# State-space projection: pairs of channel tiles by seven half products, with sums of weights and of rows

## What is computed

```python
D_INNER, SSD_HEADS, SSD_GROUPS, D_STATE, D_CONV = 2048, 32, 4, 128, 4
XBC_DIM = D_INNER + 2 * SSD_GROUPS * D_STATE      # 3072

def ssd_mixer(h, w_in, conv_w, conv_b, dt_bias, a_log, d_skip, gate_norm, w_out):
    z, xbc, dt = jnp.split(h @ w_in, [D_INNER, D_INNER + XBC_DIM], axis=-1)
    xbc = jax.nn.silu(causal_depthwise_conv(xbc, conv_w, conv_b))
    xs, bm, cm = jnp.split(xbc, [D_INNER, D_INNER + SSD_GROUPS * D_STATE], axis=-1)
    dt = jax.nn.softplus(dt.astype(jnp.float32) + dt_bias.astype(jnp.float32))
    a = -jnp.exp(a_log.astype(jnp.float32))
    y = ssd_chunked_scan(xs, dt, a, bm, cm) + d_skip[:, None] * xs
    y = y.reshape(Bsz, S, D_INNER) * jax.nn.silu(z.astype(jnp.float32))
    ...
```

## Time and profile before

| | |
|---|---|
| three runs | 2775.22 us median (2773.9 to 2781.66) |
| the profiled execution, its own time | 2773.66 us |
| its span, first to last instruction | 2771.9 us |
| mean granted clock of TensorE | 0.978 |
| PE busy over the span | 2646.5 us (95%) |
| DVE / ACT busy over the span | 1865.4 us (67%) / 1610.9 us (58%) |
| projection stage | about 1247 to 1724 us of the span |

### The profile page before, as it was taken

The page is one execution under the profiler, slowest core; times in us unless marked ns, Lnnn a source line. Parts: engine busy times, 40 slices in busy tenths (PEclk is TensorE's granted clock), DMA queues, the critical chain, the costliest instruction groups (busy, mean ns, idle before and its releaser), DMA issues. The chain is left out here.

```text
span 2771.9 us, 40341 instructions
## 1 busy us (share of the span) xinstructions
PE 2646.5 (95%) x13893; PEld 2137.9 (77%) x13893; DVE 1865.4 (67%) x2201; ACT 1610.9 (58%) x2036; POOL 543.3 (20%) x464
## 2 busy tenths in 40 slices
PE   8999999898999999999999999999998999999993
PEld 7886667676888888877788887887885888888882
DVE  6335766537888888876572542786335888888896
ACT  4135555425888888865331222784122888888883
POOL 0000000001334444420000000441000344334440
PEclk9999999998999999999999999999999999999996
DMA  4315110016999999966242323884114999999995
GB/s 167 89 46 183 40 47 24 31 71 247 378 380 379 386 389 383 383 258 208 73 124 69 122 84 133 308 304 144 46 39 157 353 391 383 371 381 379 380 373 233
DMA packets 238390, 619.23 MB, mean 223 GB/s; under 512 B 31976, under 2 KB 76544, under 8 KB 238144
## 3 DMA queue, kind: packets, MB, share of 16 engines
q1 hardware_dynamic: 206992, 558.88, 55.6%
q0 software_dynamic: 19136, 33.61, 3.2%
q10 hardware_dynamic: 12144, 25.17, 2.6%
HBM read 567.08 MB, written 86.13 MB: 236 GB/s over the span
## 5 line engine op out<-in xcount | busy, mean ns | idle before, releaser
L2680 DVE TENSOR_TENSOR moe_w_low<-moes_raw,moe_w_high 128x2048 fp32r<-128x2048 f32 x384 | 865.5, 2288 | 128.9 <-ACT moe_w_high L2609 128.9
L2609 ACT ACTIVATE moe_w_high<-moes_raw 128x2048 fp32r<-128x2048 f32 x384 | 721.8, 1915 | 52.9 <-PEq L155 39.2
L2471 POOL COPY moe_pick<-moes_tokens 128x1 int32 (+1 forms) x64 | 104.1, 1627 | 585.7 <-PE moe_px L2522 580.7
L174 PE MATMUL moe_py<-moe_w_high,moe_h_high 128*128 128x512 f32 x512 | 209.2, 409 | 0.0
L174 PE MATMUL moe_pg<-moe_w_high,moe_x_high 128*128 128x512 f32 x512 | 204.5, 399 | 0.0
L174 PE MATMUL moe_pu<-moe_w_high,moe_x_high 128*128 128x512 f32 x512 | 204.3, 399 | 0.0
L176 PE MATMUL moe_py<-moe_w_high,moe_h_low 128*128 128x512 f32 x512 | 201.1, 393 | 0.0
L176 PE MATMUL moe_pg<-moe_w_high,moe_x_low 128*128 128x512 f32 x512 | 200.9, 392 | 0.0
L176 PE MATMUL moe_pu<-moe_w_high,moe_x_low 128*128 128x512 f32 x512 | 200.8, 392 | 0.0
L175 PE MATMUL moe_py<-moe_w_low,moe_h_high 128*128 128x512 f32 x512 | 199.6, 390 | 0.0
L175 PE MATMUL moe_pu<-moe_w_low,moe_x_high 128*128 128x512 f32 x512 | 199.0, 389 | 0.0
(11 more groups left out here) (444 smaller groups left out, 6119.8 us busy)
## 6 DMA issues: line engine op xcount, KB each, us to landing
moes_raw<-in_w_gate SPq DMA_DIRECT2D x128, 1024.0 KB, 7.6
moes_raw<-in_w_up SPq DMA_DIRECT2D x128, 1024.0 KB, 7.8
moes_raw<-in_w_down SPq DMA_DIRECT2D x128, 1024.0 KB, 8.3
XC<-pre SPq DMA_DIRECT2D x24, 512.0 KB, 5.1
Z<-sproj_z SPq DMA_DIRECT2D x32, 256.0 KB, 2.4
scan_z<-Z SPq DMA_DIRECT2D x32, 256.0 KB, 6.0
YS<-scan_y ACTq DMA_DIRECT2D x32, 256.0 KB, 6.1
y_first<-YS SPq DMA_DIRECT2D x16, 512.0 KB, 3.9
```

What stands on the lines that cost most here:

```text
L174: nc.tensor.matmul(out, lh, rh, start=start, stop=False)
L2471: nc.gpsimd.tensor_copy(pick[a][:, :], M.tokens[:, bass.ds(b, 1)]).then_inc(picked[a], 1)
L2609: nc.scalar.activation(wh[c % SPLIT_SLOTS][:, :], M.raw[j][:, :], ACT.Copy).then_inc(w_high, 1)
L2680: nc.vector.tensor_tensor(wl[j][:, :], M.raw[c % RAW_SLOTS][:, :], bits(wh[j][:, :]), ALU.subtract).then_inc(w_low, 1)
```

## The change

**Seven products instead of eight.** Two tiles of channels (2p and 2p + 1) form a pair. With the contraction cut into two halves of 4 tiles (KH) and the rows into two halves, the pair's result is a 2 x 2 product of half blocks. It took eight half products (each 12 matmuls, four contraction tiles by three passes); now it takes seven, by sums of blocks (the Winograd form of Strassen's scheme). UNITS holds 12 pairs of 7 products (84 units of 12 matmuls) between two gate groups ahead (16 units) and two behind.

**Sums of rows, once.** mix(k), k = 0 to 3, on DVE: four additions that give back whole rows from high and low parts, four subtractions and two low parts, each 128 x 512; ACT makes two high parts. mix_late(j), j = 0 to 3: the high part (ACT) and low part (DVE) of 128 x 1024, into the buffers of the gate weights, free only in the last unit of gate group 1.

**Sums of weights, per pair.** ACT scales both tiles by the gains in 16 instructions of 128 x 128 (gain_tile, in place of DVE's L1472). DVE makes 4 sums (weights_sum). Each of the 7 operands, 128 x 512, gets a high part (ACT, operand_high) and a low part (DVE, operand_low), three products ahead, in a ring of 4.

**Combination, per pair.** The products go to 8 banks in turn. ACT copies the first to e1 (keep_e1), DVE adds the others up in 7 instructions of 128 x 512 (add_u2 to add_c12) into u. The first tap of a convolution is ACT's (tap_first), three stay on DVE. For 8 of the 24 tiles (LATER: the odd tile in two pairs of three) u is stored to XC instead, loaded again during the last two gate groups, and convolved there.

**Room.** acc, c, two of the raw buffers and others now lie in X. So X is stored to a new tensor XS (8 stores of 512 KB, after the additions) and loaded back in the scan (8 loads, at items 20 to 27). sums and step_to_end move from NT + 9 and NT + 12 to NT + 3 and NT + 5. first_operands is issued at NU - 3.

```diff
+    UNITS = [('gate', g, t) for g in range(EARLY) for t in range(NT)]
+    V0 = len(UNITS)
+    UNITS += [('pair', p, q) for p in range(NPAIR) for q in range(PRODUCTS)]
+    V1 = len(UNITS)
+    UNITS += [('gate', g, t) for g in range(EARLY, G) for t in range(NT)]
...
+    WHEN = {NT: range(5, 9), V1 - 4: (9,), V1 - 3: (10,), V1: (11, 12), V1 + NT - 1: range(13, 17)}
...
+    LATER = [2 * p + 1 for p in range(NPAIR) if p % 3 < 2]
...
+    PREPARE = {NT + 2: 0, NT + 4: 1, NT + 5: 2, NT + 6: 3}
...
+            for t in range(NT):
+                sp.wait_ge(added[1], t + 1)
+                sp.dma_start(K.XS[tile(t), :], K.X[:, t, :]).then_inc(x_saved, 16)
...
-                if v == NU - 4:
...
+                if v == NU - 3:
...
+            def product(v):
...
+                if p == 0 and q == 1:
+                    pe.wait_ge(late_low, 2)
+                if p == 0 and q == 3:
+                    pe.wait_ge(late_low, 4)
+                if p == 0 and q >= 4:
+                    pe.wait_ge(mix_low, 2 * KH)
+                pe.wait_ge(op_low, o + 1)
...
+                    last = split_product(nc, out, (h[:, k, :], l[:, k, :]), moving(q, k), k == 0, k == KH - 1)
...
+            def gain_tile(i):
+                act.wait_ge(raw_loaded[buffer_of(('tile', i))], 16 * loads_until(('tile', i)))
+                for k in range(ND):
+                    last = nc.scalar.activation(raw_tile(i)[:, k, :], raw_tile(i)[:, k, :], ACT.Copy, scale=K.vecs[:, V_SSD + k:V_SSD + k + 1])
+                last.then_inc(tile_gained, 1)
+            def operand_high(o):
+                p, n = divmod(o, PRODUCTS)
+                if o >= SLOTS:
+                    act.wait_ge(done, V0 + o - SLOTS + 1)
+                else:
+                    act.wait_ge(x_turned, NT)
+                if n in (0, 2, 5):
+                    act.wait_ge(tile_gained, 2 * p + 2)
+                else:
+                    act.wait_ge(s_ok, 4 * p + {4: 1, 3: 2, 1: 3, 6: 4}[n])
+                high, _ = operand(o)
+                nc.scalar.activation(high, source(o), ACT.Copy).then_inc(op_high, 1)
...
+            def mix(k):
+                for n, (high, x) in enumerate(((T1H, tmp[0]), (T4H, tmp[3]))):
+                    act.wait_ge(mixed, 2 * k + n + 1)
+                    nc.scalar.activation(high[k], x, ACT.Copy).then_inc(mix_high, 1)
...
+            def mix(k):
+                lo, hi = slice(0, HALF), slice(HALF, S)
+                def whole(out, kk, h):
+                    step(V.tensor_tensor(out, bits(K.HH[:, kk, h]), bits(K.HL[:, kk, h]), ALU.add))
+                if k:
+                    dve.wait_ge(mix_low, 2 * k)
+                whole(tmp[0], k, lo)
+                whole(tmp[1], k, hi)
+                whole(tmp[2], KH + k, hi)
+                whole(tmp[3], KH + k, lo)
+                V.tensor_tensor(tmp[0], tmp[1], tmp[0], ALU.subtract).then_inc(mixed, 1)
+                step(V.tensor_tensor(t3f[:, k, :], tmp[2], tmp[1], ALU.subtract))
+                dve.wait_ge(mixed, 2 * k + 1)
+                step(V.tensor_tensor(t2f[:, k, :], tmp[2], tmp[0], ALU.subtract))
+                V.tensor_tensor(tmp[3], tmp[3], t2f[:, k, :], ALU.subtract).then_inc(mixed, 1)
+                dve.wait_ge(mix_high, 2 * k + 1)
+                V.tensor_tensor(T1L[k], tmp[0], bits(T1H[k]), ALU.subtract).then_inc(mix_low, 1)
+                dve.wait_ge(mix_high, 2 * k + 2)
+                V.tensor_tensor(T4L[k], tmp[3], bits(T4H[k]), ALU.subtract).then_inc(mix_low, 1)
...
+            def operand_low(o):
+                dve.wait_ge(op_high, o + 1)
+                high, low = operand(o)
+                V.tensor_tensor(low, source(o), bits(high), ALU.subtract).then_inc(op_low, 1)
+            def weights_sum(p, n):
+                second, first = raw_tile(2 * p), raw_tile(2 * p + 1)
+                lo, hi = slice(0, KH), slice(KH, ND)
+                dve.wait_ge(tile_gained, 2 * p + 1 + (n > 1))
+                if n > 1:
+                    dve.wait_ge(s_ok, 4 * p + n - 1)
+                elif p == 0:
+                    dve.wait_ge(sums_stored, 32)
+                else:
+                    dve.wait_ge(op_low, PRODUCTS * (p - 1) + 5)
...
+                V.tensor_tensor(out, a, b, op).then_inc(s_ok, 1)
...
+                if v in PREPARE:
+                    mix(PREPARE[v])
...
+                if v == V0 - 1:
+                    mix_late(0)
+                    mix_late(1)
+                if v == V0:
+                    mix_late(2)
+                    mix_late(3)
+                p, s = divmod(v - V0, PRODUCTS)
+                here, ahead = 0 <= p < NPAIR, -1 <= p < NPAIR - 1
+                if s == 0 and 0 < p <= NPAIR:
+                    add_c12(p - 1)
+                if here and s == 2:
+                    add_u2(p)
+                if here and s == 4:
+                    add_u3(p)
+                if here and s == 3:
+                    add_c11(p)
+                if here and s == 5:
+                    add_u4(p)
+                    add_c22(p)
+                if here and s == 6:
+                    add_c21(p)
+                if ahead and s == 4:
+                    weights_sum(p + 1, 2)
+                if 0 <= v - V0 + 3 < NPAIR * PRODUCTS:
+                    operand_low(v - V0 + 3)
+                if ahead and s == 3:
+                    weights_sum(p + 1, 1)
+                if ahead and s == 4:
+                    weights_sum(p + 1, 3)
+                if ahead and s == 6:
+                    weights_sum(p + 1, 4)
+                for i, some in convs.get(v, ()):
+                    convolve(i, some)
...
+                if 5 * LOAD <= n < 7 * LOAD:
+                    t = n - 5 * LOAD
+                    sp.dma_start(K.X[:, t, :], K.XS[t * P:(t + 1) * P, :]).then_inc(K.x_back, 16)
```

More of the change, by code:

```diff
@@ L1123, in ssd_project_stage @@
[L1123 to L1134, removed]
@@ new lines, in ssd_project_stage @@
+    SEQ = [i for i in range(NTILES) if i not in LATER] + LATER
+    NOW = NTILES - len(LATER)
+    rank = {i: n for n, i in enumerate(SEQ)}
+    LEADS = 4
+    taps, silus, stores, convs = {}, {}, {}, {}
+    for i in SEQ[:NOW]:
+        v, row = V0 + PRODUCTS * (i // 2 + 1), i % 2
+        taps.setdefault(v, []).append(i)
+        silus.setdefault(v + 2 * (row + 1), []).append(i)
+        stores.setdefault(v + 2 * row + 3, []).append(i)
+        for n, some in enumerate(((1,), (2, 3)) if row else ((1, 2, 3),)):
+            convs.setdefault(v + row + n, []).append((i, some))
@@ new lines, in _ @@
+            load(('piece', 7))
+            load(('piece', 8))
+            sp.wait_ge(x_saved, 16 * NT)
+            sp.wait_ge(scaled, NT)
+            sp.dma_start(tap, A["conv"].rearrange("k p n -> p k n")).then_inc(tap_loaded, 16)
+            for v in range(0, NU + 2):
+                if v == NT + 1:
+                    for i in range(4):
+                        load(('tile', i))
+                if v == V1 + 2:
+                    for n in range(13, 17):
+                        load(('piece', n))
+                p, s = divmod(v - V0, PRODUCTS)
+                if s == 4 and 0 <= p < NPAIR - 2:
+                    load(('tile', 2 * p + 4))
+                    load(('tile', 2 * p + 5))
+                if s == 4 and p in (NPAIR - 2, NPAIR - 1):
+                    for n in range(2):
+                        load(('piece', 9 + n + 2 * (p - NPAIR + 2)))
+                if v == NT + 6:
@@ L1308, in _ @@
                     last.then_inc(dt_done, 1)
-                unit(v)
+                if UNITS[v][0] == 'gate':
+                    gate(v)
+                else:
+                    product(v)
                 if v == NT:
@@ L1422, in _ @@
             for v in range(NU + 2):
-                if v == NT:
-                    act.wait_ge(dt_done, 1)
-                    for h in range(2):
-                        nc.scalar.activation(dts[:, half(h)], pd[h], ACT.Copy).then_inc(dt_kept, 1)
-                if 1 <= v <= NU:
+                if 1 <= v <= NU and UNITS[v - 1][0] == 'gate':
                     evict(v - 1)
@@ new lines, in add_c12, with convolve @@
+            def add_c12(p):
+                ready(p, 6)
+                dve.wait_ge(u4_ok, p + 1)
+                V.tensor_tensor(result(p, 1, 1), bank(p, 6), result(p, 1, 1), ALU.add).then_inc(c12_ok, 1)
+            def convolve(i, taps_now):
+                r, t = rank[i], TILES[i]
+                for n in taps_now:
+                    if n == 1:
+                        dve.wait_ge(first_tap, r + 1)
+                    else:
+                        dve.wait_ge(steps, (CONV - 2) * r + n - 1)
+                    last = V.scalar_tensor_tensor(out=acc[r % 2], in0=u_at_hand(i)[:, n:n + S], scalar=tap[:, t, n:n + 1], in1=acc[r % 2],
```

442 lines of the change are left out of this document (296 added, 146 removed).

## The result

The median went from 2775.22 to 2761.39 us (five runs each side); the ratio is 0.9946, 95% interval 0.9931 to 0.9961. The forecast was 2759, and faster. The profiled execution took 2761.39, its span is 2759.4 against 2771.9, and what differs from the forecast lies at the two ends of the stage, above all at its exit.

The account below looks back on a forecast made before the run. PE (TensorE), busy 30 of 30 us mid-stage, was taken as the bound. Span 2771.9 - 32.6 + 10.2 + 2 + 4 = 2755.5; plus 1.8 (execution) and 1.56 (median) gives 2759 us; range 2744 to 2774.

Parts of the forecast that it names:

- The matmuls removed, -32.6: In the pairs' products: 84 matmuls per pair instead of 96, 144 fewer at 0.2267 us each, saving 32.6 us.
- The pairs at no cost: In the pairs: DVE's mean load of 16.2 us stays under PE's 19.04 and ACT's work is hidden; cost 0.
- Rival (c): In the pairs: DVE becomes the bound and the kernel slower, 2784 us; gain gone from 20.4 us per pair; chance 0.09.
- The handshake on every new instruction: In the pairs on DVE: 0.27 us idle at each of 18 new instructions, 4.9 us more per pair.
- The entry, +10.2 and +2 for the clock: Way into the pairs: DVE's and ACT's queues delay product 1 by 10.2 us; lower clock afterwards costs 2 us.
- rival (a): Entry and exit covered, ACT running ahead and stores sharing the rings; only 3 us lost, 2745.6 us; chance 0.14.
- The exit, +4: Way out to the scan: late first operands and last gate stores queued behind them cost 4 us, bounds 0 and 9.
- The rest at nothing: Saving x, restoring it, third gate group's splits: 0 each, up to 3, 2, 2 us; start's store stalls: 0.5 gain at most.
- The clock within the pairs: In the pairs: the granted clock was expected to hold 1.00 despite a bank change every 12 matmuls instead of 24.
- rival (d): In the pairs: PE falls to the lower clock; a fifth of the matmuls slowed gives 2799 us; chance 0.03.
- The clock behind the idle: Behind PE's idle ahead of product 1: matmuls start 0.43 us apart instead of 0.2267; 2 us, from 0 to 5.

Follow-up runs that it names:

- e8b_dve_more: Changed kernel with each operand's low part subtracted twice on DVE, 84 instructions more; median 2788.29 us, ratio 1.0047 to the kernel before.
- e1: Changed kernel without DVE's wait for the two stores of the sums ahead of pair 0's first sum of weights; median 2758.08 us against 2761.4.
- e9_none_later: Changed kernel with no convolution put behind the pairs, all 24 run in them; median 2753.40 us against 2761.4.
- e2: Changed kernel with all the scan's first operands issued earlier, at gate unit V1+8 of 16; median 2764.43 us against 2761.4.
- e6b: Changed kernel with only the broadcast of the sums issued early, behind gate unit V1+1, three row loads left in place; median 2763.59 us against 2761.4.
- e6: Changed kernel with the broadcast of the sums issued behind gate unit V1+1 and the three row loads at V1+8; median 2762.10 us against 2761.4.
- e11: Changed kernel with the scan's first operands issued behind the last gate store instead of ahead of the last three; median 2766.59 us against 2761.4.
- e4_keep_busy: Changed kernel with 56 useless small transposes on PE while it waits for product 1's operands; median 2761.51 us against 2761.4.
- e3: Changed kernel with mix(0) made ahead of the step sizes in DVE's and ACT's queues; median 2756.61 us against 2761.4.

## Why the prediction was right, and where it was not

**The matmuls removed, -32.6: right.** The page has 144 fewer. With every loss taken away the stretch is 32.9 us shorter.

**The pairs at no cost: right.** DVE's 25.7 of 30 us on the mean over the pairs (1396 to 1606) is 16.3 per pair against 16.2 reckoned, and no product but the first two waits. Rival (c), DVE as the bound, gave a load at which the gain is gone of 20.4; e8b_dve_more at 21.2 is 0.47% slower than before, which fits that point. The handshake on every new instruction, which the rival needed, did not come: it would have shown as idle of DVE between them, and e8b's pace leaves no room for it.

**The entry, +10.2 and +2 for the clock: right, link by link.** Counted from dt, mix(1) ended at 42.7 (43.0 forecast), the wait for the stores at 49.3 (49.4), product 0 started at 58.75 (58.8), product 1 at 70.1 (70.3). The slow matmuls cost 1.9. One sum in it is off as written: 11.1, eight units of 5.44 and some 2 make 56.6 and not 57.4 for product 0, but the trace bears out the 57.4 (58.75 less 1.22 of idle is 57.5). Together with the pairs this makes -20.3 against -20.4. The wait on the stores was the largest link (e1: 6.7 us of product 1's start), and rival (a), an entry covered by ACT running ahead, fell.

**The exit, +4: mis-sized, it was +9.8,** beyond the upper bound of 9; the scan's first matmul came 13.4 us behind the last gate matmul, where the prediction's own sign was 6 to 9. Two things in that step failed. First the place: I put the first operands 14 units and 1 us behind the pairs, 9.9 us ahead of PE's end. I had counted the units of the convolutions and not that a SiLU waits for the store of two convolutions before; those waits (8.20 and 5.50 in the rows above) stand in the chain that made it 5.0. Second the form: I took the broadcast and the held-up eviction as two delays that overlap, and priced the second by today's 5.65 us. They are in series, and the eviction waited 14.67. That the late convolutions are the cause is shown by e9_none_later (seam 3.60 with nothing else changed for the exit); whether by their waits or by their 8 MB it leaves open. How the 5.8 us divide between place and form the runs don't tell either. They do tell that in this crowded stretch the same 3.5 MB cost 7 to 13 us wherever they go: 10.2 with e2, 9.9 with e6b (6.2 ahead, 3.7 in the seam), 6.9 with e6, 12.9 with e11.

**The rest at nothing: mostly right.** The start of the stage was 2.9 us shorter and the rest 0.9 longer. I don't put the first down to the change: the columns "to dt" of the twelve executions which are alike in that part lie between 66.3 and 68.4. From 1256 to 1266 the granted clock was 1.00 in five of them, this one among them, and 0.83 to 0.86 in seven, as in the earlier trace rows. This luck hid half of the exit's miss: the span came out 3.9 us over the 2755.5 of the sum (+5.8 exit, -2.9 start, +0.9 rest, +0.1). The median is only 2.4 over the forecast, since the 1.56 that was added for the distance of the median from the profiled execution was nothing here: the profiled one is the median. The sum was nearer than its exit term deserved.

**The clock within the pairs: right.** A change of bank every 12 matmuls left it at 1.00 in all seven stretches from 1396 to 1606, so rival (d) fell, and with it the swinging clock which the Trainium skill (TensorE: Matmul & The Clock Gate, section "A second HAM failure mode: psum-queue depth-cycling") describes for another kernel.

**The clock behind the idle: right in size, from a row that was misread.** The prediction took the 2 us from matmuls 0.43 us apart "afterwards" to an idle of 6.49 us. In the trace of before they start 15 us behind that idle, with some 60 small transposes and idles of 1.70 and 3.00 us between, and the first four matmuls behind the 3.00 us run at full pace. So that row gives the cost of a stretch at the lower clock and not the effect of one idle, which e4_keep_busy then showed. The Trainium skill (TensorE: Matmul & The Clock Gate, section "Loop structure matters more than you think") has a wait of some 8 us as one behind which the clock is the lower one; the 8.35 us here agree. The 5.05 us of e3 had the same effect.

## What to carry to other kernels

Where an edit saves work on the bound engine, the middle of the stage pays in full, and the price is at the seams: write out each engine's queue in order there, with every wait for a buffer's store in it, and look for links in series. Work moved off an engine with room left (here 16.3 of 19.04 us) is no gift: moved to the end, with its extra stores and loads, it delayed the next stage's first transfer by more than it relieved. Before moving a large load earlier, look at what its bytes will stand in front of; less traffic helped where four other orders of the same traffic did not.

## What the runs showed of the hardware

- DVE can be busy for 97% of the time (29.3 of 30 us) and still feed PE without any idle, in a kernel whose operands are made three products ahead (e9); 2.1 us more than PE's time per pair come out as 2.1 us per pair.
- In the midst of dense matmuls an idle of PE of 3.2 us (e1) left those behind it at full pace; 5.05 us (e3) and 8.35 us (after) were each followed by eight to ten matmuls 0.43 us apart, 5.73 us (e6b) by six. With all but 2.18 us of the wait filled with small transposes (e4) none followed. In the kernel before, 3.00 us of idle behind a sparse start (1260.68) were followed by four matmuls at full pace and then eight 0.43 us apart, so the length of one idle alone doesn't decide.
- The 2 MB broadcast took 11.4 to 14.0 us to land in the thirteen profiled executions, and the eviction that needed the buffer of a 256 KB store issued behind it waited 12.1 (e6b) and 14.7 us (after), where the median store lands 4.5 us behind its issue.
